# Hybrid encoder step with sixteen experts: the experts' rows loaded by GpSimd's queue in place of SP's

## The chip, the cores and the metric

The kernel runs on one core of a Trainium2 chip. The core has a matrix engine (PE, TensorE), three engines for elementwise work (DVE is VectorE, ACT is ScalarE, POOL is GpSimd), and SP (SyncE), which only issues transfers. DMAs are issued by SP, by ACT and by GpSimd, each in a queue of its own, and all of them run on the core's 16 DMA engines. The metric is the time of one execution on the device in microseconds, lower is better, given as the median of the runs.

## The reference, cut to what matters

Two layers run over 576 tokens: 512 of a prompt and 64 of a later chunk, with D = 1024. Each layer has a mixer (sparse attention beside a convolution) and a channel mixer, which is a mixture of 16 experts in 4 groups. Every token takes the best group and in it the best two experts. Everything is float32. The change lies in the second part alone:

```
g_sel = argmax(hf @ w_router_group + b)                    # 1 of 4 groups
top_p, top_i = top_k(softmax(e_logits[g_sel]), 2)          # 2 of its 4 experts
hid = silu(hf @ w_gate[e]) * (hf @ w_up[e]) * gate[:, e]   # w_gate, w_up: (16, 1024, 256)
out = sum over e of hid @ w_down[e]                        # w_down: (16, 256, 1024)
x = x + gt_f * out
```

## The kernel before

The kernel doesn't compute all experts for all tokens. It sorts rows into `x_d`, a DRAM buffer in which each expert owns 128 rows. For each tile `t` of 128 tokens (the fifth has 64), VectorE works out the two slots of each token (`sid1`), and GpSimd scatters the tile's rows twice with an indirect DMA (`scatter`, line 1773, 10 of them, counted by `s_xs`). Then each expert `e` reads its 128 rows (512 KB) back as one tile, `xg[:, e % 2]`. There are two such buffers.

PE goes through the experts in `step` (from line 809). For expert `e` it computes the gate and up products (32 matmul instructions of 128x256, line 475), turns the rows of expert `e + 1` by eight transposes (line 485, counted by `L["tx"]`, two per expert), computes the down products of expert `e - 1` (8 instructions of 128x512), and turns the hidden values of expert `e`. ACT and DVE copy the turned rows out of PSUM, and ACT stores each expert's result to `y_d` (512 KB). GpSimd gathers from `y_d` at the end of the layer.

Weights go through a ring of six slots of 1 MB (`W`, function `load`, line 372). An expert takes three: gate, up, down. So two experts fit. A load waits until PE has released its slot (`w_free`), and SP issues the loads strictly in the order gate, up, down of expert after expert. In this stream SP also issues the row loads (`rows`, line 429): those of experts 0, 1 and 2 after the weights of expert 1, behind the wait on `s_xs`, and those of expert `e + 1` between up and down of expert `e`. A row load for expert `e` waits until the rows of expert `e - 2` have been turned.

An expert can be chosen by more than 128 tokens. The tokens beyond that go to further jobs. VectorE counts them in `tables()`, after the stage has begun, and then raises `L["ready"]`. GpSimd waits for that, reads the number of jobs (`jobs`, line 1789), and if there are any scatters all rows a second time with another table (`sid2`, 10 scatters, counted by `s_xo`). With this input layer 0 has one further job and layer 1 none. Between the two sets of scatters GpSimd issues, in layer 0 only, the 17 small loads of the next layer's vectors and caches (`vectors` and `late_loads`, lines 337 to 359).

Of the kernel before, what the change touches and what calls it, by code (L numbers as in the profile page):

```python
# [24 lines left out]
P = 128  # L25
# [9 lines left out]
NE = 16  # L35
# [63 lines left out]
def program(nc, A, O):  # L99
    ctx = ExitStack()  # L100
    with ctx:
# [73 lines left out]
        xg = part(10880, 2048, 2, D)  # L175
# [15 lines left out]
        x_d = dram("x_d", [SPARE + 2 * NT * P, D])  # L191
# [169 lines left out]
        @block.sync  # L361
        def _(sp):
            further = sp.alloc_register("sp_further")
            expert = sp.alloc_register("sp_expert")

            def load(use, src):
                slot, turn = use % 6, use // 6
                if turn > 0:
                    sp.wait_ge(w_free[slot], turn)
                n = src.shape[-1] * src.shape[-2]  # L370
                dst = W[:, slot, 0:n].rearrange("p (k c) -> p k c", c=src.shape[-1])
                sp.dma_start(dst, src).then_inc(w_ld[slot], 16)

            wada = A["w_ada"].rearrange("l (k p) c -> l p k c", p=P)
            win = A["w_in"].rearrange("l (k p) c -> l p k c", p=P)
            wout = A["w_out"].rearrange("l (k p) c -> l p k c", p=P)
            wexp = [A[n].rearrange("l e (k p) f -> l e p k f", p=P) for n in ("w_gate", "w_up", "w_down")]

            def ada(first_use, third, ks=range(KC)):
                l, q = THIRDS[third]  # L380
                for k in ks:
                    load(first_use + k, wada[l, :, k:k + 1, 2048 * q:2048 * q + 2048])

            for i in range(8):
                load(i, wada[0, :, i:i + 1, 0:2048])
            for l in range(DEPTH):
                def shifted(i):

                    sp.wait_ge(s_glu, 4 * l + i + 1)
                    if i >= 2:  # L390
                        sp.wait_ge(s_conv, 4 * l + i - 1)
                    for j in range(4):
                        for g in range(4):
                            sp.dma_start(G4[i % 2][32 * j:32 * j + 32, g, 0:634],  # L394
                                         gT[32 * g:32 * g + 32, i, j:j + 634]).then_inc(s_g4[i % 2], 16)

                for c in range(8):
                    if l == 0 and c == 3:
                        ada(U_ADA1, 0)
                        ada(U_ADA2, 1)  # L400
                    for hf in range(2):
                        ks = slice(4 * hf, 4 * hf + 4)
                        if c in (4, 5):
                            c0 = CU + 512 * hf + 256 * (c - 4)
                            src = win[l, :, :, c0:c0 + 256]
                        else:
                            w, c0, c1 = {0: (win, CIQ, CIK), 1: (win, CIK, CU), 2: (win, CK, CIQ), 3: (win, CQ, CK),
                                         6: (wout, 0, 512), 7: (wout, 512, 1024)}[c]
                            src = w[l, :, ks, c0:c1]
                        load(mixer_use(l, c, hf), src)  # L410
                    if l == 0 and c == 4:
                        ada(ada3_use(0), 2, range(2))
                    if l == 0 and c == 5:
                        shifted(0)
                        ada(ada3_use(2) - 2, 2, range(2, 6))
                        shifted(1)
                        shifted(2)
                        ada(ada3_use(2) - 2, 2, range(6, KC))
                        shifted(3)
                        ada(U_ADA4, 3)  # L420
                        ada(U_ADA5, 4)
                    if l == 1 and c == 6:
                        for i in range(4):
                            shifted(i)
                def rows(e):

                    if e >= 2:
                        sp.wait_ge(L["tx"], 2 * (e - 1))
                    sp.dma_start(xg[:, e % 2, :], x_d[e * P:e * P + P, :]).then_inc(s_xg[e % 2], 16)

                for e in range(NE):
                    for j, w in enumerate(wexp):
                        load(expert_use(l, e) + j, w[l, e])
                        if j == 1 and 2 <= e < NE - 1:
                            rows(e + 1)
                    if e == 1:
                        sp.wait_ge(s_xs, (l + 1) * 160)
                        rows(0)
                        rows(1)
                        rows(2)  # L440

                sp.wait_ge(n_cnt, l + 1)
                sp.reg_load(further, jobs[0:1, XJ:XJ + 1])
                with sp.If_ne(further, 0):
                    sp.wait_ge(L["tx"], 2 * NE)
                    sp.wait_ge(s_xo[l], 160)
                    with sp.Fori(0, sp.snap(further, min_val=0, max_val=XJ)) as x:
                        sp.dma_start(xg[:, 0, :], x_d[bass.ds(x * P + XROW, P), :]).then_inc(M["jld"], 16)
                        sp.reg_load(expert, jobs[0:1, bass.ds(x, 1)])
                        e = sp.snap(expert, min_val=0, max_val=NE - 1)  # L450
                        for s, w in enumerate(wexp):
                            sp.dma_start(JW[s].rearrange("p (k c) -> p k c", c=D if s == 2 else DE),
                                         w[l, bass.ds(e, 1)].rearrange("e p k f -> (e p) k f")).then_inc(M["jld"], 16)
                        leave(sp, "sp")
            sp.wait_ge(s_x, 32)
# [1265 lines left out]
        def _(pool):  # L1721
# [9 lines left out]
            for l in range(DEPTH):  # L1731
# [38 lines left out]
                def scatter(t, k, table, done):  # L1770

                    m = rows_of(t)
                    G.indirect_dma_start(out=x_d[:, :], out_offset=bass.IndirectOffsetOnAxis(ap=table[0:m, 5 * k + t:5 * k + t + 1], axis=0),  # L1773
                                         in_=HR[0:m, t, :], in_offset=None).then_inc(done, 16)

                pool.wait_ge(s_fill, 64)
                for t in range(NT):
                    pool.wait_ge(L["sid"], t + 1)
                    for k in range(2):
                        scatter(t, k, sid1, s_xs)  # L1780

                if l + 1 < DEPTH:
                    pool.wait_ge(s_mst, 160)
                    pool.wait_ge(L["outst"], 128)
                    vectors(pool, l + 1)
                    late_loads(pool, l + 1)
# [3 lines left out]
                with pool.If_ne(further, 0):  # L1790
                    for t in range(NT):
                        for k in range(2):
                            scatter(t, k, sid2, s_xo[l])
                pool.wait_ge(L["jdone"], 1)
                pool.wait_ge(L["yst0"], 16 * (NE // 2))
                pool.wait_ge(L["yst1"], 16 * (NE // 2))
# [40 lines left out]
```

## Time and profile before

| | |
|---|---|
| median of 3 runs | 1485.41 us (1483.56 to 1487.31) |
| profiled execution, its own time | 1487.12 us |
| its span | 1485.2 us |
| PE busy | 1255.7 us, 85% |
| DVE, ACT, POOL busy | 549.1, 363.2, 152.2 us |
| transfers | 284.99 MB, of them 42.50 MB in GpSimd's queue, 209.70 MB in SP's |

The profile is of one execution. In its timelines the first number of a line is the start in us from the start of the span and the second its length in us; "L475" is line 475 of the kernel. Brackets at the end give the idle time of the engine just before, and what ended it. "SPq" is a DMA that SP issues; its length is the time of the issue, not of the transfer. The time from an issue to its landing stands in a line of its own. All transposes are PE matmuls with line 485. Layer 0's expert stage lies at about 525 to 750 us of the span, layer 1's at about 1255 to 1452.

### The profile page before, as it was taken

The page shows a single profiled execution, that of the slowest core. Times are in us where ns is not written, and L with a number is a line of the kernel's source. Part 1 is how long each engine was busy: PE and PEld are TensorE (multiplying, and loading weights), DVE is VectorE, ACT ScalarE, POOL GpSimd, SP SyncE. Part 2 cuts the span into 40 slices and gives each one's busy share as a digit, 9 for nine tenths or more (in the row PEclk, how much of TensorE's full clock was granted, in tenths as well). Part 3 has the DMA queues.
Part 4 walks back from the last instruction along what each step waited for, and adds up shares of the span by engine and source line. Part 5 has one row for each costly group of instructions (what it writes and reads, how often), then busy time and mean ns, then how long its engine had stood idle before and what let it go on. Part 6 is the DMA issues. An engine that isn't in the chain of part 4 may idle for free.

```text
span 1485.2 us, 16192 instructions
## 1 busy us (share of the span) xinstructions
PE 1255.7 (85%) x6299; PEld 738.0 (50%) x6299; DVE 549.1 (37%) x1394; ACT 363.2 (24%) x828; POOL 152.2 (10%) x218
## 2 busy tenths in 40 slices
PE   3998799987899879999817989899787995999990
PEld 0572244543545456777504633454345454777760
DVE  1106689023235531111142048980323353311115
ACT  2114120025741111111122133001368111211111
POOL 0401050010000160000021013100100011000002
PEclk7999799997999879999968989899858997999995
DMA  9238996260960489999660320223220016699986
GB/s 361 65 133 305 371 330 198 53 248 5 317 212 29 165 277 371 364 360 361 234 234 0 113 69 29 67 53 110 67 59 21 1 58 233 208 360 365 366 295 209
DMA packets 137174, 284.99 MB, mean 192 GB/s; under 512 B 11613, under 2 KB 91909, under 8 KB 130697
## 3 DMA queue, kind: packets, MB, share of 16 engines
q1 hardware_dynamic: 116416, 209.70, 42.0%
q0 software_dynamic: 8352, 42.50, 8.2%
q10 hardware_dynamic: 12329, 31.74, 5.9%
q8 instruction: 50, 0.82, 0.2%
q14 instruction: 27, 0.22, 0.1%
HBM read 237.91 MB, written 52.40 MB: 195 GB/s over the span
## 4 chain that ended last, share of the span: by engine, by line
PE 69%; DVE 11%; DMA 8%; ACT 5%; issue 4%; SPq 1%; ACTq 1%; POOL 0%; DVEq 0%; POOLq 0%
PE ps L475 45%; PE ps L764 9%; PE ps L485 5%; PE ps L622 3%; DMA W<-in_w_gate 3%; PE ps L683 3%; ACT arena L1105 2%; DMA X<-in_x_sample 2%; SPq L394 1%; DVE arena L1409 1%; PE ps L505 1%; PE ps L583 1%; DVE arena L1460 1%; DVE arena L1370 1%; DMA arena<-y_d,sid 1%
## 5 line engine op out<-in xcount | busy, mean ns | idle before, releaser
L475 PE MATMUL ps<-W,arena 128*128 128x256 f32 (+1 forms) x1280 | 346.0, 426 | 10.0 <-DMA W<-in_w_gate 4.8
L475 PEld LDWEIGHTS ps<-W,arena 128*128 128x128 f32 x1280 | 240.9, 192 | 85.2 <-issue 55.7
L475 PE MATMUL ps<-W,hT 128*128 128x512 f32 (+5 forms) x640 | 196.1, 466 | 6.8 <-DVE gt L1289 6.8
L485 PE MATMUL ps<-C,arena 128*128 128x128 f32 (+3 forms) x851 | 124.5, 291 | 61.3 <-DMA arena<-x_d 14.5
L475 PEld LDWEIGHTS ps<-W,hT 128*128 128x128 f32 (+1 forms) x640 | 102.9, 182 | 100.0 <-issue 85.7
L764 PE MATMUL ps<-W,hT 128*128 128x512 f32 (+1 forms) x320 | 145.3, 608 | 6.6 <-ACT hT L1162 6.6
L485 PEld LDWEIGHTS ps<-C,arena 128*128 128x128 f32 (+3 forms) x851 | 102.0, 154 | 97.6 <-issue 31.8
L475 PE MATMUL ps<-hT,W 128*128 128x64 f32 (+1 forms) x512 | 142.4, 439 | 7.1 <-ACT arena L1028 7.1
L475 PEld LDWEIGHTS ps<-hT,W 128*128 128x128 f32 x512 | 78.8, 193 | 72.0 <-issue 64.2
L764 PEld LDWEIGHTS ps<-W,hT 128*128 128x128 f32 (+1 forms) x320 | 57.2, 184 | 81.2 <-issue 74.1
L1672 DVE TENSOR_TENSOR arena<-arena,ps 128x256 f32<-128x256 f32 x32 | 13.5, 421 | 216.3 <-ACT arena L1203 216.3
L1369 DVE MAX8 small<-arena 64x8 f32<-64x576 f32 (+3 forms) x132 | 80.5, 610 | 3.7
L1370 DVE MATCH_REPLACE8 arena<-small,arena 64x576 f32<-64x576 f32 (+3 forms) x132 | 78.5, 594 | 0.0
L622 PE MATMUL ps<-arena 128*32 128x64 f32 (+1 forms) x1024 | 65.0, 412 | 4.4 <-DMA arena<-arena 4.4
L1773 POOL DMA_INDIRECT x_d<-arena,sid x30 | 28.8, 960 | 381.5 <-DVE sid L1582 368.7
L505 PE MATMUL ps<-W,scT 128*32 128x512 f32 x384 | 58.5, 708 | 10.6 <-DMA W<-in_w_ada 10.2
L683 PE MATMUL ps<-arena 64*128 64x128 f32 (+4 forms) x160 | 56.7, 626 | 11.7 <-DVE small L1460 11.3
L1801 POOL DMA_INDIRECT arena<-y_d,sid x20 | 19.8, 988 | 402.5 <-DMA y_d<-arena 201.3
L1203 ACT ACTIVATE arena<-ps 128x256 f32<-128x256 f32 x32 | 12.3, 384 | 191.8 <-PE ps L475 191.8
L1105 ACT ACTIVATE arena<-arena,small 128x128 f32<-128x128 f32 (+4 forms) x80 | 47.3, 593 | 45.1 <-DVE small L1472 45.0
L1460 DVE CUSTOM_DVE_ANT_0 arena<-ps,arena 64x512 f32<-64x512 f32 (+3 forms) x64 | 35.9, 587 | 56.0 <-PE ps L683 55.3
L1667 DVE COPY arena<-ps 128x512 f32<-128x512 f32 x32 | 22.1, 691 | 93.1 <-PE ps L475 93.1
(244 smaller groups left out, 1106.7 us busy)
## 6 DMA issues: line engine op xcount, KB each, us to landing
W<-in_w_ada SPq DMA_DIRECT2D x48, 1024.0 KB, 7.0
W<-in_w_gate SPq DMA_DIRECT2D x32, 1024.0 KB, 10.7
W<-in_w_up SPq DMA_DIRECT2D x32, 1024.0 KB, 13.1
W<-in_w_down SPq DMA_DIRECT2D x32, 1024.0 KB, 7.7
arena<-x_d SPq DMA_DIRECT2D x33, 512.0 KB, 11.0
y_d<-arena ACTq DMA_DIRECT2D x33, 512.0 KB, 7.3
W<-in_w_in SPq DMA_DIRECT2D x16, 1024.0 KB, 7.0
arena<-arena SPq DMA_DIRECT2D x128, 79.2 KB, 2.1
```

Source lines behind the costliest of these rows:

```text
L475: ins = T.matmul(out, l, r, start=n == 0, stop=n == len(pairs) - 1, skip_group_check=True)
L485: count(T.transpose(o, i, ident[0:m, 0:m]), done if n == len(outs_ins) - 1 else None)
L505: ins = T.matmul(out[32 * j:32 * j + 32, :], scT[:, k, :], W[:, use % 6, 512 * j:512 * j + 512], start=k == 0, stop=k == KC - 1, skip_grou ...
L622: ins = T.matmul(ps[b][32 * g:32 * g + 32, 0:n], W4[:, i % 2, NQ * g + q, :], G4[i % 2][:, g, s0 + 4 * q:s0 + 4 * q + n], start=q == 0, st ...
L683: T.matmul(ps[logit_bank(job)][0:rows_of(t), 0:b - a], q, kT[1][hp, a:b], start=True, stop=True).then_inc(L["lgt"], 1)
L764: ins = T.matmul(ps[5 + n % 3][0:rows_of(t), :], hT[:, 4 * q + k, tokens(t)], wv[:, k, :], start=q == 0 and k == 0, stop=last, skip_group_ ...
L1105: ins = S.activation(r, r, ACT.Exp, bias=small[0:m, q:q + 1], accum_out=small[0:m, h:h + 1])
L1369: chain(V.max(m8, sc))
L1370: chain(V.match_replace(sc, m8, sc, MARK))
L1460: ins = V.tensor_tensor_reduce(r[:, 0:k], ps[logit_bank(job)][0:m, 0:k], mk[:, 0:k], 0.125, MARK, ALU.add, ALU.max, small[0:m, mx:mx + 1])
L1667: V.tensor_copy(ys[:, u, 512:1024], ps[7][:, :]).then_inc(L["yd"], 1)
L1773: G.indirect_dma_start(out=x_d[:, :], out_offset=bass.IndirectOffsetOnAxis(ap=table[0:m, 5 * k + t:5 * k + t + 1], axis=0), in_=HR[0:m, t, ...
```

## The change

`rows` moves from SP's program to GpSimd's. GpSimd waits until its ten scatters have landed, issues the rows of experts 0, 1 and 2, then the next layer's small loads (layer 0), then waits for `ready`, issues the second scatters if there are any, and then the rows of experts 3 to 15, each behind the same wait on `L["tx"]` as before. SP issues only weights.

```
@@ SP @@
-                def rows(e):
-
-                    if e >= 2:
-                        sp.wait_ge(L["tx"], 2 * (e - 1))
-                    sp.dma_start(xg[:, e % 2, :], x_d[e * P:e * P + P, :]).then_inc(s_xg[e % 2], 16)
-
                 for e in range(NE):
                     for j, w in enumerate(wexp):
                         load(expert_use(l, e) + j, w[l, e])
-                        if j == 1 and 2 <= e < NE - 1:
-                            rows(e + 1)
-                    if e == 1:
-                        sp.wait_ge(s_xs, (l + 1) * 160)
-                        rows(0)
-                        rows(1)
-                        rows(2)
@@ GpSimd @@
+                def rows(e):
+
+                    if e >= 2:
+                        pool.wait_ge(L["tx"], 2 * (e - 1))
+                    pool.dma_start(xg[:, e % 2, :], x_d[e * P:e * P + P, :]).then_inc(s_xg[e % 2], 16)
+
+                pool.wait_ge(s_xs, (l + 1) * 160)
+                for e in range(3):
+                    rows(e)
                 if l + 1 < DEPTH:
                     pool.wait_ge(s_mst, 160)
                     pool.wait_ge(L["outst"], 128)
                     vectors(pool, l + 1)
                     late_loads(pool, l + 1)
...
                     for t in range(NT):
                         for k in range(2):
                             scatter(t, k, sid2, s_xo[l])
+                for e in range(3, NE):
+                    rows(e)
                 pool.wait_ge(L["jdone"], 1)
```

SP's queue in layer 0, from the weights of expert 1 to gate of expert 3, before (`arena<-x_d` is a row load, since `xg` is a part of the buffer `arena`; `w_free` is the wait for a slot, `l_tx` the one for PE's turned rows):

```order
L372 DMA W<-in_w_gate 128x8x256 [waits w_free1]
L372 DMA W<-in_w_up 128x8x256 [waits w_free2]
L372 DMA W<-in_w_down 128x2x1024 [waits w_free3]
L429 DMA arena<-x_d 128x1024 [waits s_xs]
L429 DMA arena<-x_d 128x1024
L429 DMA arena<-x_d 128x1024 [waits l_tx]
L372 DMA W<-in_w_gate 128x8x256 [waits w_free4]
L372 DMA W<-in_w_up 128x8x256 [waits w_free5]
L429 DMA arena<-x_d 128x1024 [waits l_tx]
L372 DMA W<-in_w_down 128x2x1024 [waits w_free0]
L372 DMA W<-in_w_gate 128x8x256 [waits w_free1]
```

The same place in SP's queue after the change:

```order
L372 DMA W<-in_w_gate 128x8x256 [waits w_free1]
L372 DMA W<-in_w_up 128x8x256 [waits w_free2]
L372 DMA W<-in_w_down 128x2x1024 [waits w_free3]
L372 DMA W<-in_w_gate 128x8x256 [waits w_free4]
L372 DMA W<-in_w_up 128x8x256 [waits w_free5]
L372 DMA W<-in_w_down 128x2x1024 [waits w_free0]
L372 DMA W<-in_w_gate 128x8x256 [waits w_free1]
```

The four row loads and their waits are gone, and the weight loads keep their order and their waits.

GpSimd's queue in layer 0, from the last small loads to the end of the expert stage, before (`x_d<-arena,sid` is a scatter, `arena<-y_d,sid` the gather at the end):

```order
L358 DMA rb<-in_b_router_group 128x4
L359 DMA rb<-in_b_router_expert 128x16
L1789 TENSOR_LOAD jobs [waits l_ready]
L1790 COMPARE_AND_BRANCH
L1773 DMA x_d<-arena,sid 4352x1024 x10
L1790 UNCONDITIONAL_BRANCH
L1801 DMA arena<-y_d,sid 128x1024 [waits l_yst1,l_yst0,l_jdone]
```

The same place after the change, with line numbers of the changed kernel, from the last first-set scatter and the first three row loads on:

```order
L1760 DMA x_d<-arena,sid 4352x1024
L1773 DMA arena<-x_d 128x1024 [waits s_xs]
L1773 DMA arena<-x_d 128x1024
L1773 DMA arena<-x_d 128x1024 [waits l_tx]
L337 DMA vrows<-mod_d 16x128 [waits l_outst,s_mst]
...
L359 DMA rb<-in_b_router_expert 128x16
L1785 TENSOR_LOAD jobs [waits l_ready]
L1786 COMPARE_AND_BRANCH
L1760 DMA x_d<-arena,sid 4352x1024 x10
L1786 UNCONDITIONAL_BRANCH
L1773 DMA arena<-x_d 128x1024 [waits l_tx] x13
L1799 DMA arena<-y_d,sid 128x1024 [waits l_yst1,l_yst0,l_jdone]
```

Three row loads with two waits now stand ahead of the small loads, and the other thirteen stand behind the second scatters.

## Rows read from the trace of the kernel before

**Rows 1.** Page, chain that ended last, by line.

```profile
PE ps L475 45%; PE ps L764 9%; PE ps L485 5%; PE ps L622 3%; DMA W<-in_w_gate 3%; PE ps L683 3%; ACT arena L1105 2%; DMA X<-in_x_sample 2%; SPq L394 1%; DVE arena L1409 1%; PE ps L505 1%; PE ps L583 1%; DVE arena L1460 1%; DVE arena L1370 1%; DMA arena<-y_d,sid 1%
```

**Rows 2.** PE's waits, 524 to 730 us: total us, times, longest.

```profile
PE ps L485 <- DMA arena<-x_d: 7.2, 1, 7.2
PE ps L475 <- DMA W<-in_w_gate: 4.3, 4, 2.6
```

**Rows 3.** PE's waits, 1254 to 1452 us.

```profile
PE ps L475 <- DMA W<-in_w_gate: 0.5, 2, 0.2
```

**Rows 4.** Stretches: length, busy us by engine, PE clock, DMA share, GB/s.

```profile
583.00:712.00 129.00, 127.30 (x555) 95.31 (x554) 20.53 (x34) 21.18 (x44) 0.00 (x0) 1.00 1.04 360
...
1281.00:1284.00 3.00, 3.00 (x12) 1.57 (x10) 1.11 (x2) 1.17 (x2) 0.00 (x0) 1.00 0.00 0
...
1296.00:1435.00 139.00, 138.41 (x603) 103.54 (x602) 21.63 (x36) 23.11 (x48) 0.00 (x0) 1.00 1.05 364
```

**Rows 5.** Timeline of SP's queue in both expert stages.

```profile
545.21 0.34 SPq L429 DMA_DIRECT2D arena<-x_d  x1
557.61 0.37 SPq L372 DMA_DIRECT2D W<-in_w_down  x1
...
1286.57 5.60 SPq L429 DMA_DIRECT2D arena<-x_d  x1
...
1368.89 5.13 SPq L429 DMA_DIRECT2D arena<-x_d  x1
1377.33 0.37 SPq L372 DMA_DIRECT2D W<-in_w_down  x1
```

**Rows 6.** Timeline of PE in both expert stages.

```profile
564.43 1.04 PE L485 MATMUL ps<-C,arena 128*128 128x128 f32 x8
...
571.71 7.14 PE L475 MATMUL ps<-W,arena 128*128 128x256 f32 x32 [2.59 <-DMA W<-in_w_gate]
...
606.75 7.07 PE L475 MATMUL ps<-W,arena 128*128 128x256 f32 x32
...
618.19 7.07 PE L475 MATMUL ps<-W,arena 128*128 128x256 f32 x32
...
711.51 10.58 PE L475 MATMUL ps<-W,arena 128*128 128x256 f32 x40 [0.36 <-DMA W<-in_w_gate]
...
1280.40 1.04 PE L485 MATMUL ps<-C,arena 128*128 128x128 f32 x8
...
1296.77 7.14 PE L475 MATMUL ps<-W,arena 128*128 128x256 f32 x32 [0.24 <-DMA W<-in_w_gate]
...
1435.02 10.51 PE L475 MATMUL ps<-W,arena 128*128 128x256 f32 x40
```

**Rows 7.** Chain that ended last, in order of time, layer 0's start.

```profile
528.72 3.58 DMA arena<-x_d
...
532.35 1.97 PE ps L485 x8
```

**Rows 8.** Line 352, the 256 KB load of ck at 531.2 us, landing.

```profile
DMA to landing us min/median/max: 4.6/4.6/4.6
```

**Rows 9.** Timeline of GpSimd, layer 0's expert stage.

```profile
526.05 0.56 POOL L337 DMA_DIRECT2D vrows<-mod_d  x1
...
544.13 1.03 POOL L1773 DMA_INDIRECT x_d<-arena,sid  x1 [7.04 <-issue]
...
555.55 0.90 POOL L1773 DMA_INDIRECT x_d<-arena,sid  x1 [0.30 <-issue]
```

**Rows 10.** Timeline of DVE, the last instruction of the tables.

```profile
542.43 0.17 DVE L1657 TENSOR_TENSOR sid<-route,C 128x10 uint32<-128x10 f32 x1
```

**Rows 11.** Line 1773, the scatter issued at 544.1 us, landing.

```profile
DMA to landing us min/median/max: 7.4/7.4/7.4
```

**Rows 12.** Line 1773, scatters issued at 554.3 and 555.5 us, landing.

```profile
DMA to landing us min/median/max: 10.4/11.3/12.2
```

**Rows 13.** Page, DMA issues: count, size, median us to landing.

```profile
W<-in_w_gate SPq DMA_DIRECT2D x32, 1024.0 KB, 10.7
```

## The prediction, made before the changed kernel ran

> **What bounds the kernel now.** I read the page's chain first, to see where the end is set, then PE's waits in the two expert stages, then the DMA share by stretch, then the queues of PE, SP and GpSimd around the places that the change touches. In the chain PE's matmuls of line 475 hold 45% of the span, and the only transfer inside the expert stages that stands out is the load of the gate weights [rows 1]. In layer 0's expert stage PE waits 7.2 us for the first expert's rows and 4.3 us, in four places, for gate weights; in layer 1's it waits only 0.5 us for gate weights [rows 2, 3]. So the row loads hold PE once per layer, at the start, and never afterwards.
>
> The steady part of the stage has two bounds that lie almost on each other. An expert without a wait takes PE 618.19 - 606.75 = 11.44 us [rows 6]. In the same stretches the DMA share is 1.04 and 1.05 at 360 and 364 GB/s [rows 4]. An expert moves three weight tiles of 1.05 MB, 0.52 MB of rows in and 0.52 MB of results out, 4.19 MB, which is 11.5 us at 364 GB/s. From expert 3's first matmul to expert 15's, 12 experts, layer 0 takes 711.51 - 571.71 = 139.8 us and layer 1 1435.02 - 1296.77 = 138.25 us, against 12 x 11.44 = 137.3 us for PE alone [rows 6]. Only 2.5 and 1.0 us of the two stages is time in which DMA sets the pace. With the 2.59 and 0.24 us just ahead [rows 6], all that better feeding could give back is 5.1 + 1.2 = 6.3 us.
>
> **SP without the rows.** SP's row issue lasts 5.13 us in the row shown, because the queue behind it is full, but the next instruction, the down load, starts at 1377.33, 3.3 us after that issue is over (1368.89 + 5.13 = 1374.02) [rows 5]. What it waits for is PE's release of the slot. Gate and up of the next expert stand behind that same wait, in SP's queue before and after. Taking the rows out therefore brings no weight load forward: 0 us. At the start of the stage SP no longer waits for the scatters, but both halves of the weight buffer are full by then and gate of expert 2 waits for PE's first products anyway: 0 us too. If the down load had followed the row issue at once, the 5.13 us would have been the prize; it didn't.
>
> **The first rows, from GpSimd.** The wait on the scatters is the same; only the issuer changes. SP's load of expert 0's rows takes 3.58 us from issue to landing [rows 7]. No direct GpSimd load of 512 KB is in the trace. The nearest is the load of ck, 256 KB, 4.6 us with others around it [rows 8]. The bounds are a gain of 0.1 and a loss of 1.1 us, and I take half of the upper one, +0.5 us, since ck has four times shorter runs and neighbours. PE waits for nothing else there, so it counts in full, once per layer: +1.0 us. The Trainium skill, "DMA: Bandwidth & Descriptors", section "Latency and other measured facts", gives about 0.6 us to the first byte for a load issued by SP and about 1 us for GpSimd. By that alone the term would be +0.4 us per layer, and no run so far shows it.
>
> **Expert 3's rows in layer 0.** This is the place that decides. GpSimd now waits, ahead of 17 small loads, until PE has turned expert 0's rows. Those loads ran from 526.05 to 544.13 - 7.04 = 537.09, 11.0 us, and GpSimd then stood idle for the 7.04 us until 544.13 [rows 9]. Now the third row load is issued when PE's first turns end, at 532.35 + 1.97 = 534.3 [rows 7] plus the 0.5 us; with some 0.6 us for the issue itself the small loads run from 535.4 to 546.5. VectorE's table is ready at 542.60 [rows 10]; the ten scatters began 1.5 us behind it. With GpSimd itself late, they begin at 546.5 + 1.5 = 548.0, and take 556.45 - 544.13 = 12.3 us of GpSimd [rows 9]: expert 3's rows are issued at 560.3, where SP did it at 545.21 [rows 5]. PE wants to turn them at 564.43 [rows 6], 564.9 with the late start.
>
> How long do they take to land? They stand in GpSimd's own DMA queue behind the scatters. The first scatter landed 7.4 us after its issue, the last 12.2 us [rows 11, 12]. Below I set the bare 4.6 us of ck [rows 8], above the 12.2 us and 1.8 us for one more transfer of that size (the lag of the scatters grew by 4.8 us over nine, on top of 1.27 us apart: 1.8 us each), 14.0 us. I take 8.0 us, near the first scatter's: the scatters start later beside the weights of expert 2, no rows are in SP's queue beside them, and SP issues nothing more between its last load of that group and 557.61 [rows 5], so the backlog is smaller than before. Landing is then 568.3, a stall of 3.4 us. Behind it stand a turn, down of expert 1 and two short turns, which lasted from 564.43 to 571.71 - 2.59 = 569.12, 4.7 us. So gate products of expert 3 begin at 573.0 instead of 571.71: +1.3 us, with the start's 0.5 us already inside. The wait of 2.59 us for gate weights hides the rest of the stall. Without that cover the 3.4 us would all count. At the bounds the landing is 564.9 or 574.3, which gives +0.5 us (the late start alone) or +7.3 us.
>
> **Layer 1.** There are no small loads and no second scatters. Expert 3's rows go out when the table is ready; in layer 0 that was at 542.60 with SP's issue at 545.21 [rows 5, 10], and GpSimd's 1.5 us behind the table is no later than SP. Expert 4's wait only for PE's turn of expert 2, which ends at 1281.44 [rows 6], and DMA moves nothing from 1281 to 1284 [rows 4]. SP issued them at 1286.57, behind three weight loads [rows 5]. So 0.52 MB, 1.4 us of DMA time, moves into a hole. At most the 1.2 us above come back; I take 0.7. Layer 0 has no such hole left for rows, since expert 4's stand behind the scatters. With the late first rows layer 1 comes to 0.5 - 0.7 = -0.2 us.
>
> **Sum.** Layer 0 +1.3 us, layer 1 -0.2 us: +1.1 us. The profiled execution took 1487.12 us (span 1485.2 and 1.9 around it), so it would become 1488.2. It stands 1.7 us above the median of the three runs, 1485.41 us, which becomes 1486.5 us. A difference under 0.3%, 4.5 us, is about what can't be told from no change.
>
> **The rivals.**
> (a) Rows behind scatters, slower. In layer 0 the second scatters hold GpSimd's queue as they do now at their end, expert 3's rows land 14.0 us after issue, and expert 3's products start at 579.0: +7.3 us, with layer 1 +7.1, 1492.5 us. For it: the 12.2 us of the last scatter [rows 12]. Against it: in the trace the scatters shared DMA with these very rows, issued by SP at 545.21 [rows 5], and now don't. It turns the result to slower from a landing of about 11.5 us after issue on.
> (b) Rows beside gate weights, slower. GpSimd sends expert e+3's rows when expert e+1's have been turned, one down product ahead of SP's burst of weights, and in a queue of their own they share DMA with gate weights that land a median 10.7 us after issue [rows 13] and are wanted at about 11.0. Half of the rows' 1.4 us, less the 0.3 us of slack, is 0.4 us per expert, 24 times: +9.6 us, 1495 us. Against it: the bytes between two gate loads stay 4.19 MB, and DMA that is never idle finishes them at the same time in any order. The Trainium skill, "DMA: Bandwidth & Descriptors", section "Queues, rings and completion order", says each DMA engine goes round robin between the queues that have work. By that the rows would not wait behind weights any more, and this rival's 0.4 us per expert would be paid. No row here shows the order inside an engine.
> (c) Feeding gets better, faster. All 6.3 us come back and the first rows cost their 1.0: -5.3 us, 1480.1 us. For it: the hole in layer 1 and SP's full queue. Against it: gate loads stand behind the down load's wait as before, and 5.1 of the 6.3 us are in layer 0, where rows arrive later, not earlier.
> (d) The move changes nothing, as all rows but expert 3's come early either way: 1485.4 us. It lies within the forecast's own case.
>
> **How the numbers follow.** Forecast with (d) 0.61, (a) 0.17, (b) 0.10, (c) 0.12. The forecast alone spans 1483 to 1490.5 us: its first rows from -0.1 to +1.1 a layer, expert 3's landing from 4.6 to 11.5 us, and 1.5 us of scatter between runs. The range reaches to (c) and over most of (a), 1480 to 1493.5, and leaves out most of (b) and the edges. Faster by over 0.3%: nearly all of (c), 0.12, and a little of the forecast, 0.01. Slower: (a), (b) and the forecast's upper edge, less the part of (a) and (b) that comes out smaller, 0.25. Within: 0.62.
>
> **What the new profile would show.** Right: PE waits for x_d rows in three places, 7.5 to 8 us at each layer's start and 2 to 5 us at about 565; the wait for gate(3) is gone or under 1 us; SP's down loads still start when PE frees the slot; expert steps stay at 11.44 to 11.7 us; in layer 1 the gate waits shrink. Wrong: a wait for rows at 565 of over 6 us (a), steps of 11.9 us throughout (b), a landing of the first rows outside 3.5 to 4.7 us, waits for rows of any later expert, or a layer 0 stage shorter than before.

## The result, and the profile after

The changed kernel takes 1500.51 us in the median of 4 runs (1496.54 to 1503.54), the kernel before 1486.36 us in the runs beside it (4, 1483.56 to 1488.17). The ratio is 1.0087, with a 95% interval of 1.006 to 1.0115. It is slower, by 14 us, where 1 us was forecast. The profiled execution took 1503.54 us (span 1501.6), 16.4 us over that of before, and 3 us above its own median.

The page's chain by line, which answers to [rows 1] (line 462 is the old line 475, line 472 the old 485, since the file is 13 lines shorter up to there):

```profile
PE ps L462 38%; DMA W<-in_w_up 9%; PE ps L751 9%; PE ps L472 5%; PE ps L609 3%; PE ps L670 3%; ACT arena L1092 2%; DMA X<-in_x_sample 2%; SPq L394 1%; DVE arena L1396 1%; PE ps L492 1%; DMA arena<-x_d 1%; DVE arena L1447 1%; PE ps L570 1%; DMA arena<-y_d,sid 1%
```

The gate load is gone from the costliest entries, and the up load stands in it with 9%. PE's waits in layer 0's expert stage, as in [rows 2]:

```profile
PE ps L472 <- DMA arena<-x_d: 14.7, 2, 7.7
...
PE ps L462 <- DMA W<-in_w_up: 1.0, 3, 0.4
PE ps L462 <- DMA W<-in_w_gate: 0.4, 1, 0.4
```

There are two waits for rows now, one at the start and one of 7.1 us at expert 3. PE's timeline shows what follows (compare [rows 6]):

```profile
573.47 1.97 PE L472 MATMUL ps<-C,arena 128*128 128x128 f32 x8 [7.06 <-DMA arena<-x_d]
575.23 5.08 PE L462 MATMUL ps<-W,arena 128*128 128x512 f32 x8
580.15 0.38 PE L472 MATMUL ps<-C,arena 128*128 128x128 f32 x2
580.37 7.07 PE L462 MATMUL ps<-W,arena 128*128 128x256 f32 x32
...
721.36 10.58 PE L462 MATMUL ps<-W,arena 128*128 128x256 f32 x40 [0.38 <-DMA W<-in_w_gate]
...
1314.42 3.72 PE L462 MATMUL ps<-W,arena 128*128 128x256 f32 x16 [0.32 <-DMA W<-in_w_up]
...
1451.40 10.51 PE L462 MATMUL ps<-W,arena 128*128 128x256 f32 x40
```

The turn of expert 3's rows takes 1.97 us instead of 1.04 and the down product behind it 5.08 instead of 3.60. The next fence says why: after the 7 us without work the granted clock averages 0.65 over the following stretch (columns as in [rows 4]). Its other two lines are the steady parts of the two layers.

```profile
573.00:580.40 7.40, 6.93 (x19) 4.08 (x20) 0.74 (x2) 1.17 (x2) 0.54 (x1) 0.65 0.98 331
580.40:721.00 140.60, 139.41 (x602) 102.50 (x600) 21.73 (x37) 23.11 (x48) 5.28 (x10) 1.00 1.02 349
1310.00:1451.00 141.00, 139.42 (x601) 102.66 (x600) 21.64 (x36) 23.12 (x48) 5.28 (x10) 1.00 1.03 353
```

In the steady parts DMA moves 349 and 353 GB/s, where it was 360 and 364. GpSimd's timeline answers to [rows 9]:

```profile
537.15 0.52 POOL L337 DMA_DIRECT2D vrows<-mod_d  x1
...
548.49 1.03 POOL L1760 DMA_INDIRECT x_d<-arena,sid  x1 [0.30 <-issue]
...
559.91 0.90 POOL L1760 DMA_INDIRECT x_d<-arena,sid  x1 [0.31 <-issue]
560.81 1.15 POOL L1773 DMA_DIRECT2D arena<-x_d  x2
575.73 0.54 POOL L1773 DMA_DIRECT2D arena<-x_d  x1 [13.78 <-PE ps L472]
```

The line at 560.81 holds two issues, the rows of experts 3 and 4. Expert 3's rows landed after (line 1773, that one issue):

```profile
DMA to landing us min/median/max: 12.6/12.6/12.6
```

The page's DMA issues, with the median time to landing in the last column, for the two loads that changed (the up load's was 13.1 before, the row load's 11.0):

```profile
W<-in_w_up SPq DMA_DIRECT2D x32, 1024.0 KB, 13.9
...
arena<-x_d POOLq DMA_DIRECT2D x32, 512.0 KB, 6.5
```

**Where the 16.4 us are.** I split the profiled execution at PE's first turn of rows (`t0`), at the products of expert 3 and at those of expert 15, in each layer.

| stretch | before | after | difference |
|---|---|---|---|
| start to `t0`, layer 0 | 532.35 | 534.37 | +2.0, of it 0.45 in the wait for the first rows |
| `t0` to expert 3 | 39.36 | 46.00 | +6.6 |
| expert 3 to 15 | 139.80 | 140.99 | +1.2 |
| expert 15 to `t0` of layer 1 | 548.61 | 551.31 | +2.7, of it 0.4 in the wait for the first rows |
| `t0` to expert 3 | 36.65 | 37.75 | +1.1, slow clock in expert 0's products |
| expert 3 to 15 | 138.25 | 140.98 | +2.7 |
| the rest | 50.18 | 50.20 | 0.0 |

The 1.6 us ahead of layer 0's stage can't be an effect, since up to there the two kernels do the same. The stretch from layer 0's expert 15 to layer 1's first rows, in which only the issue of the first rows was changed, lasts 544.8 to 550.5 us in the seven profiles in which SP issues the first rows, and 549.0 to 552.4 us in the six in which GpSimd does. The ranges overlap, but the means are 2.6 us apart (548.0 and 550.6), and only some 0.5 us of that is the wait for the first rows. About 1 us of the rest is found in layer 1's mixer: PE waits there for a DMA (`arena<-arena`) for 3.8 to 4.0 us in four of the six GpSimd kernels, the changed one among them, and for 3.1 to 3.5 us in all the others, and the clock over the 6 us behind it averages 0.51 to 0.52 instead of 0.73 to 0.77. Whether the change brings this about, and where the remaining difference comes from, is open, so the other 2.3 of the 2.7 us may or may not be an effect. Expert 0's products in layer 1 run in a rising clock, and `t0` to expert 1 varies from 13.0 to 14.7 us between kernels that don't differ there. What the change did for certain is the 6.6 + 1.2 us in layer 0, the 2.7 us in layer 1 and twice 0.4 us at the starts, 11.4 us.

### The profile page after: what moved, and what is told of

Same layout as the page of the kernel before. It is cut to its first block, busy times and chain, and to the rows that moved or that the text cites. A ratio compares the mean times of both kernels' runs of the same rounds, so it can differ in the third digit from the quotient of the medians.

```text
span 1501.6 us, 16192 instructions
## 1 busy us (share of the span) xinstructions
PE 1266.2 (84%) x6299; PEld 740.8 (49%) x6299; DVE 549.0 (37%) x1394; ACT 363.3 (24%) x828; POOL 170.1 (11%) x250
## 4 chain that ended last, share of the span: by engine, by line
PE 61%; DMA 15%; DVE 11%; ACT 5%; issue 3%; SPq 2%; POOL 2%; ACTq 1%; DVEq 0%; POOLq 0%
PE ps L462 38%; DMA W<-in_w_up 9%; PE ps L751 9%; PE ps L472 5%; PE ps L609 3%; PE ps L670 3%; ACT arena L1092 2%; DMA X<-in_x_sample 2%; SPq L394 1%; DVE arena L1396 1%; PE ps L492 1%; DMA arena<-x_d 1%; DVE arena L1447 1%; PE ps L570 1%; DMA arena<-y_d,sid 1%
## 5 line engine op out<-in xcount | busy, mean ns | idle before, releaser
L462 PE MATMUL ps<-W,arena 128*128 128x256 f32 (+1 forms) x1280 | 351.6, 429 | 8.3 <-ACT arena L1198 2.8
L1659 DVE TENSOR_TENSOR arena<-arena,ps 128x256 f32<-128x256 f32 x32 | 13.5, 421 | 218.0 <-ACT arena L1190 218.0
L570 PE MATMUL ps<-arena 64*64 64x512 f32 (+3 forms) x128 | 44.1, 613 | 6.8 <-ACT arena L1015 6.8
## 6 DMA issues: line engine op xcount, KB each, us to landing
W<-in_w_gate SPq DMA_DIRECT2D x32, 1024.0 KB, 10.6
W<-in_w_up SPq DMA_DIRECT2D x32, 1024.0 KB, 13.9
```

The lines of the kernel that those rows point to most:

```text
L462: ins = T.matmul(out, l, r, start=n == 0, stop=n == len(pairs) - 1, skip_group_check=True)
L570: count(T.matmul(ps[5 + n % 3][0:rows_of(t), 0:b - a], q, kT[0][hp, a:b], start=True, stop=True), L["dots"])
```

## The experiments

In the table each number is from the profiled execution, except the ratio. "So many us over before" in the text below is the difference of the two medians; the ratio of the table is estimated from all runs, and the two can differ by up to 2 us. "Stage" is `t0` to expert 15's products.

| kernel | stage of layer 0 | stage of layer 1 | ratio to before, 95% interval |
|---|---|---|---|
| before | 179.2 | 174.9 | |
| changed | 187.0 | 178.7 | 1.0087 (1.006 to 1.0115) |
| rows 3 ahead of the scatters | 188.6 | 177.3 | 1.0109 (1.0088 to 1.0129) |
| GpSimd for rows 0 to 2 only | 182.9 | 176.3 | 1.0054 (1.0037 to 1.007) |
| ACT for rows 3 to 15, early | 184.1 | 177.3 | 1.0051 (1.003 to 1.0071) |
| GpSimd from row 4 on | 185.2 | 179.0 | 1.0064 (1.0043 to 1.0084) |
| SP, one expert earlier | 180.7 | 174.8 | 1.0007 (0.9992 to 1.0023) |
| ACT, with SP's group | 186.6 | 183.4 | 1.0091 (1.0064 to 1.0117) |
| small loads last | 193.3 | 178.3 | 1.0131 (1.01 to 1.0161) |
| gate and up first, by SP | 173.6 | 173.5 | 0.9963 (0.9948 to 0.9978) |
| GpSimd behind the up load's landing | 210.1 | 206.4 | 1.0429 (1.0405 to 1.0453) |
| changed, gate and up first | 183.3 | 173.3 | 1.0041 (1.0024 to 1.0057) |
| changed, no second scatters | 177.7 | 178.9 | 1.0023 (1.0008 to 1.0038) |

### Expert 3's rows ahead of the second scatters

```
+                rows(3)
                 pool.wait_ge(L["ready"], 1)
...
-                for e in range(3, NE):
+                for e in range(4, NE):
                     rows(e)
```

> The changed kernel with one more row load, expert 3's, ahead of the wait for the table and the second scatters; experts 4 to 15 stay behind them. Backlog theory (7 of the 14 us are expert 3's rows stuck behind the second scatters in layer 0, the clock that falls in that wait included): 6 to 8 us faster than the changed kernel, so 7 to 8 us slower than before, and PE waits for rows only once in layer 0's stage. Stream theory (the loss is spread over all experts, because GpSimd-issued rows feed worse): at most 3 us faster than the changed kernel, 11 or more above before.

1501.89 us: no gain at all. The wait for rows is gone, but PE's timeline shows another in its place:

```profile
579.04 9.85 PE L462 MATMUL ps<-W,arena 128*128 128x256 f32 x32 [8.77 <-DMA W<-in_w_gate]
```

The gate load of expert 3, issued by SP at 560.16, landed 18.6 us later; in the changed kernel it took 17.1 us from its issue at 559.75, and its wait was hidden behind the wait for rows. The backlog theory missed. The total, 15.8 us over before, lies where the stream theory put it, but for its reason only in part: layer 1's twelve steps take 140.97 us, as in the changed kernel, while the largest piece of the loss stands in this one wait. The late rows and the late gate weights stand side by side, and taking one away shows the other. The products then run at a clock of 0.65 on average, 9.85 us instead of 7.1.

### GpSimd for the first three row loads only

```
-                        sp.wait_ge(s_xs, (l + 1) * 160)
-                        rows(0)
-                        rows(1)
-                        rows(2)
...
+                pool.wait_ge(s_xs, (l + 1) * 160)
+                for e in range(3):
+                    rows(e)
```

> Only the rows of experts 0, 1 and 2 are issued by GpSimd; all later ones by SP at their place in the weights' stream, as before. Backlog theory: the scatters start later but no row load stands behind them, so only the start counts, 0.5 us per layer and perhaps the gate load of expert 3 later: +1 to +2.5 us over before. Stream theory: the same, +1 to +2.5. Rival, start theory (a late start costs a stretch of low PE clock as well, and delayed small loads and scatters hold back the weights of expert 3): +4 to +6 us over before.

9.2 us over before (8 by the ratio), 3.7 + 1.4 us of it in the two stages. The steps in both layers are those of before (126.98 and 127.04 us for eleven, 128.29 and 126.74 before). What it costs is layer 0's start: the small loads run some 11 us later and the scatters 4 us, the wait for the gate load of expert 3 grows from 2.59 to 4.98 us, and expert 3's step takes 14.4 us instead of 11.5, since the clock falls. The start theory holds in its mechanism, but its +4 to +6 us cover only the 5.1 us in the stages, not the total.

### ACT's queue for the rows of experts 3 to 15

```
                         turned_x(e + 1, 1 - u)
+                    if e + 3 < NE:
+                        act.wait_ge(L["tx"], 2 * (e + 2))
+                        act.dma_start(xg[:, (e + 3) % 2, :], x_d[(e + 3) * P:(e + 3) * P + P, :]).then_inc(s_xg[(e + 3) % 2], 16)
```

> Rows of experts 3 to 15 are issued by ACT's queue, at the moment at which GpSimd could (right behind the turn of the expert two before); experts 0 to 2 by SP as before. Expert 3's are issued ahead of the second scatters. If the loss per expert comes from GpSimd's software queue: equal to before or 1 to 3 us faster, since rows use the hole in layer 1, steps of 11.5 us. If it comes from rows sharing DMA with weights from a queue of their own and too early: +4 to +6 us over before, steps of 11.75 us as in the changed kernel, with waits for up weights.

PE's waits in layer 0's stage show the up loads again, though no row load is issued by GpSimd:

```profile
PE ps L473 <- DMA W<-in_w_gate: 5.7, 3, 4.8
...
PE ps L473 <- DMA W<-in_w_up: 1.1, 4, 0.3
```

The total is 7.9 us over before, 2 us more than the second theory had. Its steps of 11.7 us came out: from expert 3 to 15 layer 1 takes 140.68 us, as the changed kernel (140.98), and not 138.25. So GpSimd as issuer, and its software queue, are not what costs.

### GpSimd from expert 4 on, SP before

```
-                        if j == 1 and 2 <= e < NE - 1:
+                        if j == 1 and e == 2:
...
+                for e in range(4, NE):
+                    rows(e)
```

> Rows of experts 0 to 3 by SP as before, experts 4 to 15 by GpSimd behind the second scatters: the changed kernel's steady part alone. Backlog theory alone: no PE wait for rows after the first, equal to before within 1.5 us. Stream theory: steps of 11.7 to 11.8 us in both layers at 349 to 355 GB/s, +3 to +6 us over before.

8.3 us over before, 2 us more than the stream theory had. Its steps came out: layer 1 takes 141.22 us for twelve. In layer 0 the wait for the gate load of expert 3 is 5.04 us though scatters and first rows are where they were: expert 4's rows, sent at 555.68 beside it, are what is new there. After that wait:

```profile
573.30:580.00 6.70, 6.70 (x18) 5.43 (x19) 0.00 (x0) 0.00 (x0) 0.00 (x0) 0.56 1.06 385
```

The clock column reads 0.56, close to the lower of the two levels (1.2 of 2.4 GHz), for 6.7 us; behind the kernel before's wait of 2.59 us it stayed at 1.00.

### SP, one expert earlier in its stream

```
-                        if j == 1 and 2 <= e < NE - 1:
-                            rows(e + 1)
+                        if j == 1 and e == 2:
+                            rows(3)
+                        if j == 1 and 2 <= e < NE - 2:
+                            rows(e + 2)
```

> All rows by SP in the weights' own queue, but from expert 4 on one expert earlier in the stream: behind the up load SP waits for PE's next turn and issues the rows of two experts ahead, about 3.6 us before it can issue the down load. So the moment is that of the changed kernel and the queue that of before. Own-queue theory (rows cost time because they share the DMA engines with weights from a second queue): steps as before, 11.5 us, PE's wait for the gate load of expert 3 about 2.6 us, total within 2 us of before. Earliness theory (0.5 MB of rows moved ahead of gate and up weights delays them, whatever the queue): steps of 11.7 us and waits for up weights, gate load of expert 3 waited for by 4.5 to 5 us with a slow-clock stretch behind it, +6 to +9 us over before.

```profile
PE ps L477 <- DMA W<-in_w_gate: 3.7, 2, 3.2
```

The same as before within the interval. The rows go out at the moment at which the changed kernel sends them, but in the weights' own queue, and the steps stay as before: 127.49 us for eleven in layer 0, 138.16 us for twelve in layer 1. Earliness is not the cause either; the second queue is.

Expert 5's step in layer 1 shows it in this kernel and in the one with ACT's queue. In both, SP issues down, gate and up at 0.1, 0.5 and 1.0 us after the step's first product, and the row load goes out at 7.98. In SP's queue the up load lands at 13.9 and the rows behind it at 15.2. In ACT's queue the rows land first, at 14.3, and the up load at 15.2, where PE wants it at 15.0. Over layer 1's steps the up load lands a median 12.9 us after its issue here, 14.2 with ACT's queue and 14.0 in the changed kernel; the gate load lands after 10.4, 10.6 and 10.6. In layer 0 one thing misses the expectation: the wait for expert 3's gate load is 3.2 us instead of 2.6, the clock falls, and the step takes 13.2 us.

### ACT's queue, with SP's group of loads

```
                         y_half(e - 1, 1 - u)
+                    if e + 3 < NE:
+                        act.wait_ge(L["tx"], 2 * (e + 2))
+                        act.dma_start(xg[:, (e + 3) % 2, :], x_d[(e + 3) * P:(e + 3) * P + P, :]).then_inc(s_xg[(e + 3) % 2], 16)
```

> Rows of experts 3 to 15 in ACT's queue, but issued later than in the other ACT kernel: behind the store of a result, at the moment at which SP issues its group of weight loads. A second queue, without the 3.6 us head start. Own-queue theory: steps of 11.7 us, up weights waited for, +6 to +9 us over before. Earliness theory: steps of 11.5 to 11.6 us, loss under 4 us in all.

11.5 us over before: a second queue costs here too, but more than the +6 to +9 us of the expectation, and in waits for gate weights where it had up weights. Twelve steps in layer 1 take 144.11 us, the largest steady loss so far. PE's waits in layer 1's stage:

```profile
PE ps L473 <- DMA W<-in_w_gate: 6.6, 6, 1.8
```

The gate load now lands a median 12.0 us after its issue, where it was 10.7 in that layer before. Sent 3.6 us earlier the same rows delayed the up load, which PE wants 3.5 us after gate; sent with the group they delay gate itself.

### Small loads behind expert 4's rows

```
                 for e in range(3, NE):
+                    if e == 5 and l + 1 < DEPTH:
+                        pool.wait_ge(s_mst, 160)
+                        pool.wait_ge(L["outst"], 128)
+                        vectors(pool, l + 1)
+                        late_loads(pool, l + 1)
                     rows(e)
```

> The changed kernel with the 17 small loads of layer 0 moved behind the row loads of experts 3 and 4, so that the second scatters start when the table is ready, as before, and expert 3's rows are issued some 4 us earlier. If the small loads' place is what makes expert 3's rows late: PE's second wait for rows shrinks from 7.1 us to 2 to 4 us, 3 to 6 us faster than the changed kernel (the clock stays up if the wait is short). If the weights of expert 3 are the later ones anyway (as with rows of expert 3 sent first): the wait goes over to the gate load, and the total stays within 2 us of the changed kernel.

```profile
PE ps L472 <- DMA arena<-x_d: 11.0, 2, 7.6
PE ps L462 <- DMA W<-in_w_gate: 9.9, 4, 8.8
```

The wait for rows shrinks as the first case said (11.0 - 7.6 = 3.4 us), and the gate load behind it is waited for by 8.8 us: issued at 562.44, it lands 23.2 us later, where it took 17.1 us in the changed kernel. The small loads now run beside it as well, and expert 3's rows go out only 2.4 us earlier, counted from `t0`, not 4. 1507 us, 20 us over before, a miss for both expectations on the total. The 17 loads are small, but by this run not free beside a load that PE wants next.

### Gate and up of the next expert ahead of down, by SP

```
-                for e in range(NE):
-                    for j, w in enumerate(wexp):
-                        load(expert_use(l, e) + j, w[l, e])
-                        if j == 1 and 2 <= e < NE - 1:
-                            rows(e + 1)
...
+                def weight(e, j):
+                    load(expert_use(l, e) + j, wexp[j][l, e])
...
+                for e in range(2, NE):
+                    weight(e, 0)
+                    weight(e, 1)
+                    if e + 1 < NE:
+                        rows(e + 1)
+                    if e > 2:
+                        weight(e - 1, 2)
+                weight(NE - 1, 2)
```

> A candidate for a faster version, all rows by SP: from expert 2 on SP issues gate and up of the next expert, whose slots come free earlier, ahead of down of the present one. If the head of SP's queue (the down load's wait for PE) is what keeps the gate load of expert 3 and the hole in layer 1 as they are: PE's wait for gate weights goes in both layers, 4 to 7 us faster than before. If the DMA engines are simply full: within 2 us of before.

1481.14 us, 6.3 us under the kernel before in its runs beside it: the version that beats both. PE waits for no weights of an expert in either layer, and the clock is full throughout:

```profile
568.00:705.00 137.00, 137.00 (x601) 103.06 (x599) 21.65 (x36) 23.16 (x48) 0.00 (x0) 1.00 1.05 376
1291.00:1429.00 138.00, 138.00 (x604) 103.53 (x603) 21.64 (x36) 23.16 (x48) 0.00 (x0) 1.00 1.01 353
```

Each stage of twelve steps takes 137.24 us, which is PE alone. Layer 0's DMA moved 376 GB/s here, so the 360 of before was no ceiling: what held the gate loads was the down load at the head of SP's queue, waiting for PE.

### GpSimd, each load behind the landing of an up load

```
                         pool.wait_ge(L["tx"], 2 * (e - 1))
+                    up = expert_use(l, e - 1) + 1
+                    pool.wait_ge(w_ld[up % 6], (up // 6 + 1) * 16)
```

> Rows of experts 0 to 4 by SP at their places as before, experts 5 to 15 by GpSimd, but each only once the up load of the expert before has landed, so that no row load runs beside gate or up weights that PE wants next. Own-queue theory in the form that the runs now support (a second queue takes its share of the DMA engines from the weights that PE waits for): the waits for up weights go, layer 0's gate load of expert 3 is waited for by 2.6 us as before, but rows now run beside the down and gate loads of SP's next group, so steps of 11.5 to 12.0 us; 0 to +6 us over before, less than with rows sent beside the group of SP (+13 us). If the mere number of queues costs: +6 us or more.

A miss by far: 62 us over before. Most of PE's waits in layer 0 are for rows,

```profile
PE ps L492 <- DMA arena<-x_d: 19.7, 7, 4.2
PE ps L482 <- DMA W<-in_w_gate: 5.7, 4, 2.4
```

and about half of those of 2.3 to 2.9 us, and all longer ones, lower the clock again. The up load lands too late to release a row load that PE wants within the same step, and DMA stands idle in between (303 GB/s from 600 to 711 us). It shows that a wait chosen wrong is dearer than the contention that it avoids, and nothing on the number of queues.

### The changed kernel, with gate and up first

```
-                for e in range(NE):
-                    for j, w in enumerate(wexp):
-                        load(expert_use(l, e) + j, w[l, e])
...
+                for e in range(2, NE):
+                    weight(e, 0)
+                    weight(e, 1)
+                    if e > 2:
+                        weight(e - 1, 2)
+                weight(NE - 1, 2)
```

> The changed kernel's row loads, all by GpSimd, with SP's order of the faster version: gate and up of the next expert ahead of down of the present one. If the own queue costs only because gate and up weights land just in time: with weights a whole step ahead the waits for weights go and steps are 11.44 us in both layers; what is left is expert 3's rows in layer 0 behind the scatters (wait of 6 to 9 us with its slow clock), so 2 to 5 us over before and 8 to 10 us over the faster version. If the second queue costs by itself: 8 us or more over before, steps of 11.6 us or more.

5.1 us over before, just above the 2 to 5 us of the first case, where the changed kernel is 14 us over. The steps are PE's own in both layers, with all rows in GpSimd's queue:

```profile
577.00:713.00 136.00, 136.00 (x597) 102.51 (x596) 21.32 (x36) 23.16 (x48) 5.31 (x10) 1.00 1.02 360
1301.00:1438.00 137.00, 137.00 (x600) 102.99 (x599) 21.65 (x36) 23.16 (x48) 5.31 (x10) 1.00 1.01 352
```

What is left is layer 0's expert 3: its rows, issued at 557.12, land 12.8 us later, PE waits 6.8 us, and the clock falls. So the second queue costs only where the weights land just in time, and having the rows behind the scatters costs by itself.

### The changed kernel without the second scatters

```
-                with pool.If_ne(further, 0):
-                    for t in range(NT):
-                        for k in range(2):
-                            scatter(t, k, sid2, s_xo[l])
...
-                    sp.wait_ge(s_xo[l], 160)
```

> The changed kernel without the second set of ten scatters (layer 0's further job then reads rows that were never written, that part of the computation is left out) and without SP's wait for them. If the 6.6 us of layer 0 come from the scatters in GpSimd's queue: no wait for rows or gate weights at expert 3, its products start 37 us after the first turn instead of 46.0, clock 1.00 from there on; 8 to 11 us faster than the changed kernel, while layer 1's steps stay at 11.7 us. If they come from the row loads being GpSimd's as such: the wait stays.

```profile
PE ps L471 <- DMA arena<-x_d: 7.8, 1, 7.8
PE ps L461 <- DMA W<-in_w_gate: 1.3, 3, 0.6
PE ps L461 <- DMA W<-in_w_up: 1.2, 4, 0.3
```

Expert 3's rows go out at 547.22 and land 7.8 us later. Its products begin 36.2 us after `t0`, with no wait for rows or gate weights and at full clock; the total is 9 us under the changed kernel, within the 8 to 11 us of the first case. From there layer 0 takes 141.5 us for twelve steps and layer 1 140.9, as the changed kernel does. The two parts of the loss are apart: the scatters ahead of expert 3's rows in layer 0, the second queue in the steps of both layers.

## Why the prediction was wrong, point by point

**SP without the rows: right.** SP's down load still starts when PE frees the slot, and no weight load came forward. The two kernels with gate and up first show the other half of that step, which the prediction held in its hands and didn't draw: the down load at the head of the queue was itself the bound, and moving it, not the rows, was worth 6 us.

**The first rows: right.** 7.68 and 7.65 us of waiting instead of 7.24 and 7.23, +0.4 us per layer against +0.5 taken. The size was right, but only half of it is the load itself: it landed 3.8 us after its issue instead of 3.6, and GpSimd issued it 0.29 us after the last scatter's landing where SP did so after 0.02. The Trainium skill's 0.4 us between the two kinds of issue ("DMA: Bandwidth & Descriptors", section "Latency and other measured facts") is a time to the first byte; from issue to landing this case shows 0.2 us.

**Expert 3's rows: the issue right, the landing mis-sized, and the cover wrong.** The forecast had the issue at 560.3; it was 560.81, 1.6 us of it the late start of the whole stage. The landing was taken as 8.0 us, near the first scatter's, and was 12.6, near rival (a)'s 14.0. This is the first step that failed: "near the first scatter's", because "the backlog is smaller than before". The last two scatters landed 11.4 and 11.8 us after issue, against 10.4 and 12.2 before: no smaller a backlog. Without the second scatters the same rows landed after 7.8 us. The sign that the prediction had set for rival (a), a wait for rows of over 6 us, came: 7.06 us. Two things that the sum didn't have come on top. After a wait of 7 us the clock falls, and turn, down and turn last 580.37 - 573.47 = 6.9 us instead of 4.7, +2.2. And "the wait of 2.59 us for gate weights hides the rest of the stall" took the gate load's landing as fixed. It wasn't: it took 17.1 us instead of 13.5 and would have held PE to about 577 by itself, which the first experiment shows. In all, `t0` to expert 3 grew by 6.6 us, where the sum had 0.8.

**Layer 1, and rival (b): the second step that failed.** The forecast had -0.7 us for a load in the hole; it came out at +2.7 us over twelve steps, 0.23 us each, and +1.2 us in layer 0. Rival (b) had put 0.4 us on a step and 0.10 on itself, by round robin between queues. Its cause was right and its weight wasn't; its price was too high, 0.4 us against 0.23 in layer 1 and 0.10 in layer 0 (whose steps had 2.5 us of waits before), and it named the gate load where the early rows delay the up load. The argument against it was "DMA that is never idle finishes them at the same time in any order". The order matters because PE waits for one load by name. That SP then can't issue the next group before PE has moved on, so that DMA isn't kept full, is my reading of the following count. In layer 1's twelve steps 26 of 276 half-microseconds moved less than 310 GB/s before, 44 of 281 in the changed kernel, 57 of 288 with ACT's rows beside the group; DMA is less full the more PE is made to wait. In one queue the rows stood behind the up load, where nobody wanted them yet. The Trainium skill's rule of round robin between queues ("DMA: Bandwidth & Descriptors", section "Queues, rings and completion order") agrees with the pair that differs in the queue alone: 138.16 us with SP's queue, 140.68 and 140.98 us with ACT's and GpSimd's, at the same moment of issue within 0.4 us. So does the order of landing: the rows behind the up load in SP's queue, ahead of it in ACT's and GpSimd's.

**What isn't settled.** Why the gate load of expert 3 lands later still (18.6 us) once expert 3's rows are out of the way was not taken apart; expert 5's rows, sent at 566.9 instead of 575.7, are a candidate that no run isolates. The 11.4 us that the stretches show for certain fall short of the median's 14 us; the interval of the ratio, 9 to 17 us, holds both, and the 2.3 us ahead of layer 1's stage that the profiles leave open would about close the gap. That the 17 small loads, 11 us later than before, are what holds up the gate load of expert 3 is likely from the kernels with GpSimd for rows 0 to 2 only and with the small loads last, but the scatters move with them in the one and the rows in the other.

## What to carry to other kernels

A queue is a priority list. Moving a load that isn't urgent out of the queue in which it stood behind the urgent ones gives it a share of the DMA engines at once, and with weights that land just in time every step pays. Before moving a load off a queue, look at what its head waits for: here the cure was to let loads with an early free slot pass the one with a late slot. And where a stall is removed or added, look for the second load that lands beside the first, and for the clock: a stall can be paid again in slow products.

## What the hardware showed that I had not expected

The length of a wait alone doesn't tell whether PE's clock falls behind it. These are the turns behind two waits for rows, the first in the kernel with GpSimd behind the up load's landing, the second in the one with the small loads last:

```profile
651.72 1.97 PE L492 MATMUL ps<-C,arena 128*128 128x128 f32 x8 [2.34 <-DMA arena<-x_d]
```

```profile
572.37 1.09 PE L472 MATMUL ps<-C,arena 128*128 128x128 f32 x8 [3.36 <-DMA arena<-x_d]
```

Behind 2.34 us of waiting the granted clock was 0.5 and the turn took 1.97 us; behind 3.36 us it was 1.00 and the turn took 1.09. In the expert stages of the thirteen profiles the waits from 2.3 to 3.4 us came out both ways: 1.00 behind 2.4 (twice), 2.6 (twice), 2.7, 2.9 and 3.4 us, lower behind 2.3, 2.5, 2.9 (three times), 3.2 (twice) and 3.3 us. Behind every wait of 3.8 us or more it fell. What it costs on top of the wait: expert 3's step, 11.5 us at full clock, took 13.2 and 13.5 us behind waits of 3.2 and 3.3 us, 12.9 and 14.4 us behind those near 5, and 14.2 us behind 8.8. So that is 1.4 to 2.9 us, and the longest wait did not cost the most.
